# Projection of a hybrid encoder: q, z, k and v in one phase, with the fp32 sums of squares two jobs behind their product

## What is computed

```
h = rmsnorm(x, norm1_g);  proj = h @ w_in              # 1024 -> 3600 columns: b, c, h, q, k, v, z, ab
y_a = rmsnorm_per_64(b * conv3(c * h))                 # gated convolution, 512 wide
q, k, v = silu(conv3(q)), silu(conv3(k)), silu(conv3(v))   # 4 heads of 128, depthwise, 3 taps
q = l2norm(q) / sqrt(128);  k = l2norm(k);  z = silu(z)
```

## Time and profile before

| | |
|---|---|
| median of 3 runs (lowest to highest) | 2905.53 us (2900.6 to 2908.06) |
| the profiled execution, and its span | 2908.92 us, 2907.2 us |
| PE, PEld busy, share of the span | 2624.7 us (90%), 2308.5 us (79%) |
| DVE, ACT, POOL busy | 1832.7, 989.0, 1195.4 us |
| projection, first product to last | 72.4 to 906.6 us |
| matmuls of the projection's products | 4176, in three groups of 1392 |

### The profile page before, as it was taken

The page is one execution under the profiler, slowest core; times in us unless marked ns, Lnnn a source line. Parts: engine busy times, 40 slices in busy tenths (PEclk is TensorE's granted clock), DMA queues, the critical chain, the costliest instruction groups (busy, mean ns, idle before and its releaser), DMA issues. The chain is left out here.

```text
span 2907.2 us, 44661 instructions
## 1 busy us (share of the span) xinstructions
PE 2624.7 (90%) x14945; PEld 2308.5 (79%) x14946; DVE 1832.7 (63%) x2197; ACT 989.0 (34%) x2102; POOL 1195.4 (41%) x876
## 2 busy tenths in 40 slices
PE   4999999999995999999979995698999999999991
PEld 3998998998983899999968885586787888878770
DVE  6356465564561777777763334879867766688783
ACT  6044153252362344343332222232233333323233
POOL 3111110100102756657632220366656665666660
PEclk6999999999997999999999997899999999999995
DMA  5011111111112222222124445389578677787777
GB/s 167 10 66 59 37 55 45 44 56 36 53 42 75 81 66 59 80 67 64 47 97 145 144 144 217 114 299 331 165 231 290 225 231 229 235 301 239 229 263 276
DMA packets 223040, 408.17 MB, mean 140 GB/s; under 512 B 14408, under 2 KB 103736, under 8 KB 222904
## 3 DMA queue, kind: packets, MB, share of 16 engines
q1 hardware_dynamic: 207624, 350.91, 34.6%
q0 software_dynamic: 15296, 55.59, 8.1%
HBM read 326.01 MB, written 80.44 MB: 140 GB/s over the span
## 5 line engine op out<-in xcount | busy, mean ns | idle before, releaser
L467 PE MATMUL project_proj<-hT_high,project_w_high 128*128 128x412 f32 (+3 forms) x1392 | 496.4, 357 | 27.8 <-POOL project_w_low L446 9.5
L467 PE MATMUL project_proj<-hT_low,project_w_high 128*128 128x412 f32 (+3 forms) x1392 | 475.0, 341 | 0.0
L467 PE MATMUL project_proj<-hT_high,project_w_low 128*128 128x412 f32 (+3 forms) x1392 | 474.8, 341 | 0.0
L1847 PE MATMUL experts_h<-experts_w_high,experts_xT_high 128*128 x832 | 338.9, 407 | 21.2 <-DVE experts_w_low L1747 12.5
L1747 DVE TENSOR_TENSOR experts_w_low<-experts_w_whole,experts_w_high 128x2048 fp32r<-128x2048 f32 x128 | 335.1, 2618 | 4.4
L1847 PE MATMUL experts_h<-experts_w_low,experts_xT_high 128*128 x832 | 333.9, 401 | 0.0
L1847 PE MATMUL experts_h<-experts_w_high,experts_xT_low 128*128 x832 | 328.8, 395 | 0.0
L467 PEld LDWEIGHTS project_proj<-hT_high,project_w_high 128*128 128x128 f32 (+1 forms) x1392 | 261.4, 188 | 44.8 <-issue 30.7
L444 POOL CAST project_w_high<-project_w_whole 128x1024 fp32r<-128x1024 f32 x28 | 30.3, 1081 | 637.7 <-DMA project_w_whole<-in_w_tiles_dram 637.7
L467 PEld LDWEIGHTS project_proj<-hT_low,project_w_high 128*128 128x128 f32 (+1 forms) x1392 | 261.4, 188 | 14.4 <-issue 9.8
L1745 DVE CAST experts_w_high<-experts_w_whole 128x2048 fp32r<-128x2048 f32 x128 | 199.8, 1561 | 113.2 <-DMA experts_w_whole<-in_w_dram 112.9
(11 more groups left out here) (294 smaller groups left out, 5358.0 us busy)
## 6 DMA issues: line engine op xcount, KB each, us to landing
experts_w_whole<-in_w_dram SPq DMA_DIRECT2D x128, 1024.0 KB, 8.5
experts_w_whole<-in_w_dram SPq DMA_DIRECT2D x32, 2048.0 KB, 13.5
delta_qkv<-feat SPq DMA_DIRECT2D x36, 768.0 KB, 4.9
project_w_whole<-in_w_tiles_dram SPq DMA_DIRECT2D x28, 512.0 KB, 4.2
feat<-project_out SPq DMA_DIRECT2D x48, 205.0 KB, 1.9
x_rows<-output_x SPq DMA_DIRECT2D x19, 512.0 KB, 6.4
xn_rows<-output_xn SPq DMA_DIRECT2D x19, 512.0 KB, 6.5
normalise_x<-in_x_dram SPq DMA_DIRECT2D x18, 512.0 KB, 3.6
```

The costliest lines, as they stand in the source:

```text
L467: r = pe.matmul(dst, w[s][:, kt, 0:m], x[:, kt, lo:hi], start=kt == 0 and i == 0, stop=kt == KD - 1 and i == 2)
L1847: m = pe.matmul(out[:, :], x[p][:, kt, :], w, start=kt == 0 and i == 0, stop=kt == KD - 1 and i == 2)
```

## The change

The two phases are made one. Per chunk the order is now z, q, the sum of k one chunk back, k, v, the sum of q of this chunk (at chunk 0: q, the sum of b of chunk 5, z, k, v, the sum of q). So the sum of q comes behind k and v of its own chunk, and the sum of k behind v, z and q. ACT and DVE follow the same order, `silu` of k moves ahead of `to_raw` of v, and the numbering of banks, buffers and sums is made to fit. After the last chunk PE does v, the sum of q and the sum of k, one after the other.

On SP the four loads for the next g all move into chunk 5 of the joint phase: c is loaded when z of chunk 5 is done, h when k is, b when v is, and q after the store of q; before, q and c were loaded between the two phases, h and b in the last chunk of the second. POOL splits them in that order (c, h, b, q instead of q, c, h, b).

```diff
+        def behind(c):
+            return ("k", c - 1) if c else ("b", NC - 1)
...
# SP
                 for c in range(NC):
-                    store(*(("q", c - 1) if c else ("b", NC - 1)), g)
+                    last = c == NC - 1 and more
+                    if last:
+                        load("c", g + 1, ("z", g))
                     store("z", c, g)
-                if more:
-                    load("q", g + 1, ("q", g))
-                    load("c", g + 1, ("z", g))
-                for c in range(NC):
-                    if c == NC - 1 and more:
+                    if last:
                         load("h", g + 1, ("k", g))
-                    store(*(("k", c - 1) if c else ("q", NC - 1)), g)
-                    if c == NC - 1 and more:
                         load("b", g + 1, ("v", g))
+                    store(*behind(c), g)
                     store("v", c, g)
+                    store("q", c, g)
+                    if last:
+                        load("q", g + 1, ("q", g))
                 store("k", NC - 1, g)
# POOL
-                for i, j in enumerate("qchb"):
+                for i, j in enumerate("chbq"):
# PE
                 for c in range(NC):
+                    if c:
+                        job("z", c, g)
                     job("q", c, g)
-                    sums(*(("q", c - 1) if c else ("b", NC - 1)), g)
-                    job("z", c, g)
-                for c in range(NC):
+                    sums(*behind(c), g)
+                    if not c:
+                        job("z", c, g)
                     job("k", c, g)
-                    sums(*(("k", c - 1) if c else ("q", NC - 1)), g)
                     job("v", c, g)
+                    sums("q", c, g)
                 sums("k", NC - 1, g)
# ACT
                 for c in range(NC):
+                    if c:
+                        to_side("z", c, g)
                     to_raw("q", c, g)
-                    roots(*(("q", c - 1) if c else ("b", NC - 1)), g)
-                    to_side("z", c, g)
+                    roots(*behind(c), g)
+                    if not c:
+                        to_side("z", c, g)
                     silu("q", c, g)
                     square("q", c, g)
-                for c in range(NC):
                     to_raw("k", c, g)
-                    roots(*(("k", c - 1) if c else ("q", NC - 1)), g)
+                    silu("k", c, g)
                     to_raw("v", c, g)
-                    silu("k", c, g)
+                    roots("q", c, g)
                     square("k", c, g)
                     silu("v", c, g)
                 roots("k", NC - 1, g)
# DVE
                 for c in range(NC):
                     conv("q", c, g)
-                    norm(*(("q", c - 1) if c else ("b", NC - 1)), g)
-                for c in range(NC):
+                    norm(*behind(c), g)
                     conv("k", c, g)
-                    norm(*(("k", c - 1) if c else ("q", NC - 1)), g)
                     conv("v", c, g)
+                    norm("q", c, g)
                 norm("k", NC - 1, g)
```

More of the change, by code:

```diff
@@ L336, in unit @@
         def unit(j, c):
-            return {"c": 3 * c, "h": 3 * c + 1, "b": 3 * c + 2, "q": 3 * NC + 2 * c, "z": 3 * NC + 2 * c + 1,
-                    "k": 5 * NC + 2 * c, "v": 5 * NC + 2 * c + 1}[j]
+            if j in "chb":
+                return 3 * c + "chb".index(j)
+            return 3 * NC + 4 * c + ("zqkv" if c else "qzkv").index(j)
         def item(j, c):
-            return {"b": c, "q": NC + c, "k": 2 * NC + 2 * c, "v": 2 * NC + 2 * c + 1}[j]
+            return c if j == "b" else NC + 3 * c + "qkv".index(j)
         def norm_no(j, c):
-            return "bqk".index(j) * NC + c
+            return c if j == "b" else NC + 2 * c + "qk".index(j)
         def silu_no(j, c):
             return item(j, c) - NC
+        def behind(c):
+            return ("k", c - 1) if c else ("b", NC - 1)
         def geometry(c):
```

## The result

| | before | changed |
|---|---|---|
| median of 5 runs (lowest to highest) | 2905.53 us (2900.6 to 2908.06) | 2919.19 us (2916.22 to 2919.79) |
| the profiled execution, its span | 2908.92 us, 2907.2 us | 2919.31 us, 2917.6 us |
| first to last product of the projection | 72.4 to 906.6 us | 72.9 to 916.5 us |
| from the first job of a g to that of the next | 200.9, 199.9, 200.2 us | 204.0, 204.2, 204.6 us |

The change makes the kernel slower: the ratio is 1.0048, with a 95% interval of 1.0035 to 1.006, that is +13.7 us at the medians. The forecast was +16.0 and 2921.5 us.

A forecast was written before the change was run, and what follows sets the result against it. PE was taken to bound the projection; three ends of a g +16.7, the fourth +0.7, the last job +0.3, small waits -1.7 gave +16.0: 2924.9 us, or 2921.5 on the median's scale, range 2907 to 2929.

The forecast's parts named there:

- The turn of the loop: Where the projection's loop over g starts its next pass: PE idles 2.65 to 3.7 us, change bounded at -1 to +1.

## What to carry to other kernels

Distance between a product and the sum that needs it helps only where the sum waits; here that was 1.7 us of idle time at the one short chunk, 3.8 with what a wait costs around it. Before two phases are joined, write down the last three steps of the joint phase on each engine, with everything that is moved there: the new end of the phase has one place for all that used to stand at two ends. An engine with little to do, as POOL with its 11 us in 104, can still set the end if its work falls on the few vector instructions that the last step waits for. Here one wait that put it a few us later took 16.5 us off the changed kernel's median; the second buffer with its new order took 6.8.

## What the runs showed of the hardware beyond that

The turn of the loop isn't a constant. It idles PE 2.6 to 2.9 us behind a wait of 3.5 to 8.25 us, 2.5 to 3.7 behind one of 2.65, and 3.8 to 4.3 behind one of 1.45. From the end of the last matmul ahead of that wait (v5, or S(q5) in the joint phase) to the first job of the next g it is never under 5.9 us in any trace here, whatever S(k5) does. No row names what it waits for; that stays open, and so does how much a kernel without the turn would gain.
